# A hybrid decoder layer on one core: row panels kept in DRAM as two parts, the gate panel split at the turn, rows loaded ahead of the first panel, constants later, stores of the FFN's input by SyncE

## The reference, cut to what matters

```python
D_MODEL, SEQ, WINDOW, D_FF = 1024, 2048, 128, 2816
hn = rmsnorm(h, g_attn_norm)
z = hn @ w_in                       # 512 q, 128 k, 128 v, 512 pooling channels
q, k, v, u = split(z); q, k = rmsnorm(q, g_q), rmsnorm(k, g_k)     # per head of 64
a = sliding_window_sink_attention(q, k, v, sinks, rel_bias)        # 8 query heads, 2 kv heads
m = multiscale_pool_mixer(u, w_pool, pool_scale)                   # trailing means of 2, 4, 8, 16
h = h + concatenate([a, m]) @ w_out
hn = rmsnorm(h, g_ffn_norm)
h = h + (silu(hn @ w_gate) * (hn @ w_up)) @ w_down
gate = sigmoid(rmsnorm(h, g_ple_norm) @ w_ple_gate)
h = h + gate * (p @ w_ple_proj)
```

## Time and profile before

| | |
|---|---|
| three runs | 2102.95, 2105.85, 2106.06 us; median 2105.85 |
| profiled execution | 2101.83 us, of which span 2100.0 |
| PE busy | 2060.4 us (98%) in 9802 matmuls |
| DVE, ACT, POOL busy | 1386.2 (66%), 947.6 (45%), 306.3 us (15%) |
| granted PE clock, mean | 0.998 |
| DMA | 253.44 MB, mean 121 GB/s |

### The profile page before, as it was taken

The page is one execution under the profiler, slowest core; times in us unless marked ns, Lnnn a source line. Parts: engine busy times, 40 slices in busy tenths (PEclk is TensorE's granted clock), DMA queues, the critical chain, the costliest instruction groups (busy, mean ns, idle before and its releaser), DMA issues.

```text
span 2100.0 us, 26622 instructions
## 1 busy us (share of the span) xinstructions
PE 2060.4 (98%) x9802; PEld 1702.8 (81%) x9802; DVE 1386.2 (66%) x1905; ACT 947.6 (45%) x1528; POOL 306.3 (15%) x450
## 2 busy tenths in 40 slices
PE   6999999999999999999999999999999999999998
PEld 5878778787788888888888888788888888888887
DVE  3576766767696556566688664876556566987653
ACT  3485674677663333333333453533333333333532
POOL 2443333343230000000000010000000000000100
PEclk9999999999999999999999999999999999999999
DMA  7433345343672232233916017632232227442143
GB/s 184 128 80 91 101 106 147 110 131 101 208 232 92 66 108 68 81 96 113 334 60 196 25 51 211 180 102 75 69 108 69 79 97 276 150 157 75 41 130 100
DMA packets 199244, 253.44 MB, mean 121 GB/s; under 512 B 15291, under 2 KB 128612, under 8 KB 197836
## 3 DMA queue, kind: packets, MB, share of 16 engines
q1 hardware_dynamic: 183344, 207.20, 33.6%
q0 software_dynamic: 13248, 42.53, 5.7%
q10 hardware_dynamic: 2524, 2.02, 0.4%
HBM read 203.44 MB, written 49.82 MB: 121 GB/s over the span
## 4 chain that ended last, share of the span: by engine, by line
PE 72%; DVE 1%; issue 0%; DMA 0%; ACT 0%; SPq 0%; POOL 0%; ACTq 0%
PE bank L2390 13%; PE bank L2394 13%; PE bank L2392 13%; PE bank L2452 7%; PE bank L2453 7%; PE bank L2454 7%; PE bank L2079 4%; PE bank L2081 4%; PE bank L2080 4%; PE bank L2107 1%; DMA raw<-in_w_ple_gate 0%; DVE w_lo L1396 0%; PE bank L2416 0%; ACT w_hi L918 0%; DVE a_lo L1693 0%
## 5 line engine op out<-in xcount | busy, mean ns | idle before, releaser
L2390 PE MATMUL bank<-a_hi,ring_hi 128*128 128x512 f32 x1232 | 480.4, 390 | 0.3 <-DVE h_last L1602 0.2
L2394 PE MATMUL bank<-a_hi,ring_lo 128*128 128x512 f32 x1232 | 479.4, 389 | 0.0
L2392 PE MATMUL bank<-a_lo,ring_hi 128*128 128x512 f32 x1232 | 479.3, 389 | 0.0
L2390 PEld LDWEIGHTS bank<-a_hi,ring_hi 128*128 128x128 f32 x1232 | 231.2, 188 | 49.0 <-issue 0.8
L2392 PEld LDWEIGHTS bank<-a_lo,ring_hi 128*128 128x128 f32 x1232 | 231.3, 188 | 48.1
L2394 PEld LDWEIGHTS bank<-a_hi,ring_lo 128*128 128x128 f32 x1232 | 231.2, 188 | 48.0
L2452 PE MATMUL bank<-d_hi 128*128 128x512 f32 x616 | 240.8, 391 | 0.0
L2454 PE MATMUL bank<-d_hi,d_lo 128*128 128x512 f32 x616 | 239.8, 389 | 0.0
L2453 PE MATMUL bank<-d_lo,d_hi 128*128 128x512 f32 x616 | 239.7, 389 | 0.0
L1396 DVE TENSOR_TENSOR w_lo<-raw,w_hi 128x1024 fp32r<-128x1024 f32 x111 | 140.9, 1270 | 143.5 <-ACT w_hi L918 142.5
L1236 ACT ACTIVATE d_hi<-keep 128x1024 fp32r<-128x1024 f32 x132 | 139.7, 1060 | 201.3 <-PE bank L2454 184.2
(11 more groups left out here) (238 smaller groups left out, 3821.0 us busy)
## 6 DMA issues: line engine op xcount, KB each, us to landing
hidden_T<-hid POOLq DMA_DIRECT2D x88, 256.0 KB, 2.3
raws<-in_w_gate SPq DMA_DIRECT2D x84, 256.0 KB, 4.7
raws<-in_w_up SPq DMA_DIRECT2D x84, 256.0 KB, 5.2
raw<-in_w_in SPq DMA_DIRECT2D x78, 256.0 KB, 3.9
keep<-hidden_T SPq DMA_DIRECT2D x66, 256.0 KB, 3.8
raw<-in_w_out SPq DMA_DIRECT2D x64, 256.0 KB, 4.1
raw<-in_w_ple_gate SPq DMA_DIRECT2D x64, 256.0 KB, 4.2
keep<-in_w_down SPq DMA_DIRECT2D x44, 256.0 KB, 4.4
```

Source lines behind the costliest of these rows:

```text
L2390: mm(dst[:, :], wh[:, g, cols], a_hi[o][:, k, :], start=fresh and k == 0, stop=False, skip_group_check=True)
L2392: mm(dst[:, :], wh[:, g, cols], a_lo[o][:, k, :], start=False, stop=False, skip_group_check=True)
L2394: ins = mm(dst[:, :], wl[:, g, cols], a_hi[o][:, k, :], start=False, stop=k == 3, skip_group_check=True)
```

## The change

Panels 10 to 27 (those of z(1) and out(0), one set of the 18) are loaded and split as before, and SP also stores both parts of each to DRAM (`w_split`, two DMAs of 512 KB), ahead of the load that takes over its buffers. ACT's next high part of that buffer waits for the store too. Panels 28 to 71 are not loaded raw and not split: POOL loads both parts (`load_parts`, two DMAs of 512 KB) into one of three slots made of the bytes of `raw`, `w_hi` and `w_lo`, two panels ahead, written into POOL's list at every even half; PE waits for the landing. SP's list has no panel loads there any more, but `store_n2`: for block 2 in out(3) behind the halves that copy, so ahead of the `load_a` of the same c, and for block 3 all eight behind `load_pair` 1. At the start SP loads all rows first, then panel 0; ACT squares all four pieces before it splits panel 0, PE transposes three pieces before its first half, and the constants are awaited in half 4, the band's copy in half 6. In `ple_section` panel `ple + 7` is split after the second tanh of the first column half and no longer behind the fourth. The very last 128x512 of the output is drained in two halves, and the last column half's rows are stored by SP.

```diff
+KEPT_FROM, SPLIT_END, SLOTS_W = 10, 28, 3
...
+        def has_parts(i):
+            return SPLIT_END <= i < ROW_PANELS
+        def split_of(i):
+            return min(i, SPLIT_END) + max(i - ROW_PANELS, 0)
+        def parts_slot(i):
+            return (i - SPLIT_END) % SLOTS_W
         def panel_raw(i):
             return (raw if i < ROW_PANELS else raw2)[:, i % 2, :]
         def panel_hi(i):
+            if has_parts(i):
+                return w_parts[parts_slot(i)][:, 0, :]
             return (w_hi if i < ROW_PANELS else w2_hi)[:, i % 2, :]
         def panel_lo(i):
+            if has_parts(i):
+                return w_parts[parts_slot(i)][:, 1, :]
             return (w_lo if i < ROW_PANELS else w2_lo)[:, i % 2, :]
...
+        def drained(n):
+            return [slice(0, T // 2), slice(T // 2, T)] if n == 8 * NT - 1 else [slice(0, T)]
...
         @block.sync
         def _(sp):
+            def store_parts(i):
+                sp.wait_ge(lo_done, i + 1)
+                for part, src in enumerate((panel_hi(i), panel_lo(i))):
+                    sp.dma_start(w_split[i - KEPT_FROM, part], src.bitcast(F32)
+                                 ).then_inc(parts_stored[i % 2], 16)
+            def load_z(t, c):
+                if t < 2:
+                    load(Z_AT[t] + c, z_panel(c))
+                elif t == 2 and c == 0:
+                    store_parts(SPLIT_END - 2)
+                    store_parts(SPLIT_END - 1)
+            def load_out(t, c):
+                if t == 0:
+                    load(OUT_AT[t] + c, out_panel(c))
             def load(i, halves):
                 if i in (ple_at(0), ple_at(0) + 1, ple_at(2), ple_at(2) + 1):
                     sp.wait_ge(sums4, FPAIRS * ((i - ROW_PANELS) // (2 * PLE_P) + 1))
                 elif i >= 2:
-                    sp.wait_ge(lo_done, i - 1)
+                    sp.wait_ge(lo_done, split_of(i) - 1)
+                if KEPT_FROM <= i - 2 < SPLIT_END:
+                    store_parts(i - 2)
                 for dst, src in panel_parts(i, halves):
                     sp.dma_start(dst, src).then_inc(landed[i % 2], 16)
...
             for c in range(10):
-                if c:
-                    load(Z_AT[0] + c, z_panel(c))
+                load(Z_AT[0] + c, z_panel(c))
...
             for t in range(NT - 1):
                 for c in range(10):
-                    load(Z_AT[t + 1] + c, z_panel(c))
+                    load_z(t + 1, c)
+                    for half in (2 * c - 2, 2 * c - 1):
+                        if t and half in N2_AT:
+                            store_n2(t - 1, *N2_AT[half])
                     if t and c == 3:
                         store_h1(t - 1)
                     if t == 0 and c in (7, 8):
...
                     if t == 2 and c >= 9:
                         load_h(2, 0)
                 for c in range(8):
-                    load(OUT_AT[t] + c, out_panel(c))
+                    load_out(t, c)
                     if t < 2 and c >= 6:
                         load_x_stage(t + 2, c - 4)
                     if t == 1 and c == 1:
...
             for c in range(8):
-                load(OUT_AT[3] + c, out_panel(c))
+                load_out(3, c)
+                for half in (2 * c, 2 * c + 1):
+                    if half in N2_LAST_AT:
+                        store_n2(2, *N2_LAST_AT[half])
                 if c == 3:
                     load_a(0, 0)
                     load_a(0, 1)
...
                     store_h1(3)
                 load_pair(half, 1)
                 load_a12_again(half)
+                if half == 0:
+                    for b in range(NB):
+                        for e in range(2):
+                            store_n2(3, b, e)
                 for c in range(2, FPAIRS):
                     load_pair(half, c)
                 late_half(half)
+            for j in range(NB):
+                t, b = late_block(NT - 1, j)
+                for piece, cols in enumerate(drained(8 * (NT - 1) + 4 + j)):
+                    sp.wait_ge(ple_out, 8 * (NT - 1) + 4 + j + piece + 1)
+                    sp.dma_start(out_block(t, b, 1)[:, cols], h2[(NT - 1) % 2][:, j, T + cols.start:T + cols.stop]
+                                 ).then_inc(last_stored, 16)
         @block.gpsimd
         def _(pool):
...
 +            def load_parts(i):
+                kept = (10 + i - OUT_AT[1] if OUT_AT[1] <= i < Z_AT[3] else i - Z_AT[2] if i < Z_AT[3] else
+                        i - Z_AT[3] if i < OUT_AT[2] else 10 + (i - OUT_AT[2]) % 8)
+                if i == SPLIT_END:
+                    pool.wait_ge(lo_done, SPLIT_END)
+                elif i < SPLIT_END + SLOTS_W:
+                    pool.wait_ge(panel_used, SPLIT_END)
+                    for parity in range(2):
+                        pool.wait_ge(parts_stored[parity], 16 * (SPLIT_END - KEPT_FROM))
+                else:
+                    pool.wait_ge(panel_used, i - SLOTS_W + 1)
+                pool.wait_ge(parts_stored[kept % 2], 32 * (kept // 2 + 1))
+                for part in range(2):
+                    pool.dma_start(w_parts[parts_slot(i)][:, part, :], w_split[kept, part]
+                                   ).then_inc(parts_landed[parts_slot(i)], 16)
...
-                    if t >= 2 and half in N2_AT:
-                        store_n2(t - 2, *N2_AT[half])
             def out_section(t):
                 for half in range(16):
+                    if t == 0 and half == 14:
+                        load_parts(Z_AT[2])
+                    if t and half % 2 == 0 and OUT_AT[t] + half // 2 + 2 < ROW_PANELS:
+                        load_parts(OUT_AT[t] + half // 2 + 2)
                     if t < 2:
                         if half in (0, 1):
                             powers(NORM1[t + 2], half)
...
                     if t == 3:
                         if half < 4:
                             powers(NORM2[2], half)
-                        if half in N2_LAST_AT:
-                            store_n2(2, *N2_LAST_AT[half])
                     hosted("o", t, half)
             def store_hid(half, c, j):
...
                 if half == 0:
                     for b in range(NB):
                         powers(NORM2[3], b)
-                    for b in range(2):
-                        store_n2(3, b, 0)
-                        store_n2(3, b, 1)
                 for c in range(FPAIRS):
                     if c:
                         store_hid(half, c - 1, 3)
...
-                if b == 1:
-                    pool.wait_ge(hi_done, 1)
-                    nc.gpsimd.tensor_tensor(panel_lo(0), panel_raw(0), panel_hi(0).bitcast(F32),
-                                            ALU.subtract).then_inc(lo_done, 1)
+            pool.wait_ge(hi_done, 1)
+            nc.gpsimd.tensor_tensor(panel_lo(0), panel_raw(0), panel_hi(0).bitcast(F32),
+                                    ALU.subtract).then_inc(lo_done, 1)
...
-                act.wait_ge(landed[i % 2], 32 * (i // 2) + 32)
+                if has_parts(i):
+                    return
+                act.wait_ge(landed[i % 2], 32 * (split_of(i) // 2) + 32)
                 if i >= 2:
                     act.wait_ge(panel_used, i - 1)
+                if KEPT_FROM <= i - 2 < SPLIT_END:
+                    act.wait_ge(parts_stored[i % 2], 32 * ((i - 2 - KEPT_FROM) // 2 + 1))
                 nc.scalar.activation(panel_hi(i), panel_raw(i), ACT.Copy).then_inc(hi_done, 1)
             def sum_squares(norm, b, src, junk):
...
+                            nc.scalar.activation(buf[:, cols], bank[(BS1, BS0)[e][b]][:, cols], ACT.Tanh,
+                                                 scale=0.5).then_inc(sig, 1)
+                        if e == 0 and b == 1:
+                            split(ple + 7)
             def load_constants():
                 act.dma_start(rel_sb[0:N_BUCKETS, :], rel_bias).then_inc(consts, 16)
...
             for b in range(NB):
                 act.wait_ge(first_x[b], 16)
                 sum_squares(NORM1[0], b, h[:, b, :], squares)
-                if b == 1:
-                    split(0)
+                if b == 2:
                     norm_hi(0, bank[4], wide_hi, 0, 0)
                     norm_hi(1, bank[5], wide_hi, 1, 0)
-                if b >= 2:
-                    for e in range(2):
-                        i = 2 * b - 2 + e
-                        norm_hi(i, bank[4 + i % 4], wide_hi, e, b - 1)
+            split(0)
+            for i in range(2, 6):
...
                             norm_lo(12 + b, bank[4 + b], (wide_hi, wide_lo), 1, b)
                     if half in Z_SPLIT_AT[t > 0] and not late:
                         split(Z_AT[t] + Z_SPLIT_AT[t > 0][half])
-                    if t == 0 and half == 1:
+                    if t == 0 and half == 4:
                         constants()
...
                 for e in range(2):
                     for r in range(4):
                         i = ple + 2 + 4 * e + r
```

(21 more changed lines are left out.)

87 lines of the change are left out of this document (52 added, 35 removed).

## The result

The changed kernel is slower: 2120.6 us median of four runs (2118.9 to 2124.87) against 2105.95 for the kernel before, timed beside it (2102.95 to 2107.96). The ratio is 1.0077, with a 95% interval of 1.0058 to 1.0096. The forecast of slower holds, and 2120.6 lies in the whole range (2095 to 2127), but over the forecast's own 2106 to 2119: the step is 14.7 us where 5.7 were summed, about two and a half times as much. The profiled execution took 2119.11 us with a span of 2117.0, so it is 17.0 longer than that of before, which was 4.0 under its median.

A forecast was written before the change was run, and what follows sets the result against it. PE, busy 98% of the span, was taken to bound the kernel. Gains of 17.9 and losses of 23.6 made 5.7 us slower: 2101.83 + 5.7 + 4.0 (median over profiled execution) = 2111.5 us, range 2095 to 2127.

The forecast's parts named there:

- The start: Up to panel 2: earlier first product, two waits gone, piece 2's transposes moved; 6.8 us gained (5 to 8.5).
- z(2) to out(3): z(2), z(3), out(1) to out(3): 44 splits leave ACT and DVE, so PE idles less; 7.7 us gained (3 to 12.5).
- Stores and the way into z(2): z(1), out(0): part stores lose 0.8 us (0 to 3); z(2)'s begin: POOL's first loads lose 1.2 (0 to 4).
- The FFN's operands: End of out(3) into the FFN: operand and pair 0 loads stand behind stores on SP; 21.6 us lost (10 to 28).
- The 1.6 for the fourth block's low parts: Second half of pair 0 in the FFN: the fourth operand block's low parts on DVE come late; 1.6 us lost.
- The clock's 3.5: Around the FFN's start: two idle stretches of 5 to 7.5 us cost PE clock; 3.5 us lost (0 to 6).
- The turn: Turn of the FFN: the 2.52 us wait for the earlier-split panel's low part goes; 2.6 us gained (2.4 to 2.7).
- The tail: Kernel's end: half of the last drain and SP's quicker store issue save 0.8 us (0.3 to 1.2).
- The cheap turn of out(3): Rival at out(3)'s end: operands are in time, their loss is 9.5 us, not 21.6; time 2099.4, chance 0.27.
- POOL's late loads: Rival for panels 28 to 71: some POOL loads land late and PE waits; 8 to 9 us lost, 2120, chance 0.14.
- that the splits did not matter: Rival for z(2), z(3): PE did not wait for splits, so nothing is gained there; 2118 us, chance 0.12.
- the four signs of being wrong: z(2) to FFN: PE waits for landed parts; block 3 copies delaying PE over 5 us; pair 0 before operands; copies before high parts.

The follow-up runs named there:

- Experiment 9: Changed kernel with SP's operand loads, pair 0's loads and block 3's stores reordered, plus POOL's band rows and bias loads moved into z(0): 2098.66 us, ratio 0.9975.
- experiment 6: Changed kernel with SP's operand loads, pair 0's loads and block 3's stores reordered, plus POOL's bias wait and loads moved to half 17 of z(0): 2094.85 us.
- experiment 12: Changed kernel with SP's list reordered and block 0's residual store paced, plus constants early, band's rows ahead of block 1's squares, bias in half 17: 2096.27 us.
- Experiment 10: Kernel before with the new start, constants, gate split and tail, but all 72 panels loaded raw and split, pieces stored by POOL: 2097.05 us, ratio 0.9968.
- experiment 7: Changed kernel with SP's operand loads, pair 0's loads and block 3's stores reordered, plus gate panel's split back behind the fourth tanh: 2096.2 us, ratio 0.9958.

## Why the prediction was right, and where it was not

**The start, 6.8 forecast, 3.1 at the end of z(0).** Three of the four terms held: the waits of 1.30 and 2.01 went, and with piece 2's transposes they made 6.1 by the begin of panel 2, where 5.0 were summed. The 1.8 of an earlier first product did not come (19.15 against 19.17). The row of ACT answers to the earlier trace rows:

```profile
15.61 1.06 ACT L1004 ACTIVATE w_hi<-raw 128x1024 fp32r<-128x1024 f32 x1 [0.94 <-DMA raw<-in_w_in]
```

Panel 0's high part starts at 15.61 where I took 14 to 14.5 from 237 GB/s; it had been 15.62. The other 3.0 were given back in z(0). I costed the later constants at their gain alone and did not look for what stands behind them: the band's rows (128 copies of 8 rows of 383 numbers, 1.6 MB in pieces of 1.5 KB) are written from 49.37 on, a little later than before (48.53), while PE is there 5 us earlier, and panels that share the queues with them arrive behind PE. They were no faster before: the halves issued between 50 and 70 took 3.8 to 11.0 us there and 3.6 to 11.1 here. What the earlier start used up was their slack. Experiment 9 shows that this is the place, experiments 6 and 12 that taking one wait away lets another appear.

**z(2) to out(3), 7.7 forecast, 8.4 measured** (from +0.6 to -7.8). The size and the mechanism hold. The windows answer to the earlier trace rows:

```profile
236.00:256.00 20.00, 18.27 (x128) 15.47 (x127) 15.24 (x40) 14.33 (x38) 11.82 (x19) 1.00 0.53 190
374.00:394.00 20.00, 18.55 (x131) 15.79 (x130) 14.02 (x36) 14.28 (x37) 11.50 (x21) 1.00 0.59 207
```

DVE is 2 and 1 us less busy, PE stands idle 1.7 and 1.5 instead of 3.6 and 2.1, and the clock of z(3) is 1.00 instead of 0.93. Of the 1.7 in z(2), 1.46 are the wait for panel 30, which is another matter; the two waits around the attention steps there, 1.69 and 1.29 before, are gone, and in z(3) 1.69 has become 0.88. Experiment 10, without the parts, gains nothing in this stretch.

**Stores and the way into z(2), 2.0 forecast, 3.7 measured** (from -3.1 to +0.6). z(1) and out(0) lost 1.8, with a wait of 1.26 for a low part at 204.49, and experiment 10 without these stores lost nothing there; the way into z(2) lost 1.9, of which 1.46 is the wait for a landing. I had the parts in mind that POOL loads, and not SP's store, which nothing held back any more.

**The FFN's operands, 21.6 forecast, 25.7 measured.** The chain is the one that was written down, in time shifted by the gain of 7.8: the operand loads at 562.8 (571 less 7.8 is 563.2), the third block 14 us after its issue (13.5), half 12 later by 6.2 (5.1), pair 0 at 591.1 (590.2). Two terms were too small, and one did not come. The first FFN product was 15.5 late, not 12.6: pair 0 was issued 0.9 later than written down, and its first blocks took 7.3 us from the issue to the high part at 598.41, where I took 5.2. The 1.6 for the fourth block's low parts did not come: PE has no wait between 600.78 and 630.41. The copy in the first FFN pair was 6.9 late, not 4.3; the first store of block 3 stands at 21.1 after the FFN's start, and ACT's copy needs its landing. The clock's 3.5 held: of the 5.5 above, 2.0 lie inside the 15.5, and 1.5 and 2.0 behind it. The 0.4 given back is there too.

The Trainium skill ("TensorE: Matmul & The Clock Gate", section "HAM oscillation — how this bites in real kernels") has TensorE fall back to half clock when it waits for a DMA, so that the work behind the wait starts slow. The trace agrees at all three waits, each of which goes back to a landing: the granted clock behind them is 0.52, 0.61 and 0.54. For shorter waits the profiles differ: behind the 2.52 us at the turn in the kernel before no loss of clock is seen, behind 2.79 at the same place in experiment 7 there are eight matmuls at half rate, 1.6 us.

**The turn, 2.6 forecast, 0.1 measured.** The wait went and others of the same size came behind it. What failed is to take "The low part stood behind a sum of DVE and now stands ahead of it" as the end of the matter: in this execution the second FFN half began with waits that made up for it, and in ten of the other eleven profiled kernels with the split 0.2 to 2.3 of the gain was left.

**The tail, 0.8, and 0.8 measured.**

**The rivals.** The cheap turn of out(3) needed the third block by 580; it was there at 578.7 in a kernel 7.8 ahead, which is 586.5 on the old time, 6 too late. POOL's late loads did not happen. Its 88 issues took 527 to 638 ns and landed in 4.7 us in the median, and one wait of PE in 44 panels ended at them. The Trainium skill ("SBUF — State Buffer", section "SBUF: two separate sides") has such loads held up while DVE holds the port that both share. By it they would have been late in z(2) and z(3) whenever DVE held that port; the trace shows no late issue, and which of DVE's operations here hold the port no run tells. And that the splits did not matter is refuted by z(2) and z(3), with and without the parts. That the measured 2120.6 is the 2120 of rival 2 is chance: its mechanism did not happen.

**The signs.** Of the four signs of being wrong that were written down, two came: a wait of PE for landed parts (one, 1.46 us), and a copy of block 3's pieces that keeps PE waiting for more than 5 us (6.89). The second is the term of 4.3 that was too small. The other two did not come.

So the sum as it was written and as it is: gains 17.9 and 12.4 (3.1, 8.4, 0.1, 0.8), losses 23.6 and 29.4 (3.7, 25.7); net 5.7 and 17.0, the difference of the spans. Of the 11.3 between them 5.5 are gains that did not last and 5.8 losses that were larger. The direction came from the one large term. The gains were read as if what stands behind a removed wait were in time; the losses are larger mainly by two landings, those of pair 0's first blocks and of block 3's first store.

## What to carry to other kernels

Before stores are moved to a queue, write down for each what it waits for, and put nothing behind it that is needed before that happens; two kinds of transfer whose due times cross need either two queues or an order by due time, and here that order alone was worth 26 us. When loads leave a queue, what stood behind them slides forward and may meet other transfers. An earlier stage gains no more than the slack of the transfers that have fixed times behind it: look at which of them had none left. And one profiled execution tells the order of events but not a difference of 2 us: one execution of the same lists ended z(0) some 5 us behind seven others.
